# Spreading a short convolution, halving the gates and adding a residual on TensorE in a hybrid decoder step

## The reference, cut to what matters

```
proj = h @ w_in                                  # per token: a conv part (3 x 512) and an RWKV part
y_cv = bg * conv3(cg * hv)                       # short gated convolution, three taps
y_rw = rwkv7(...)                                # a state of 8 heads x 64 x 64, step by step over the tokens
h1   = layer_norm(ALPHA * h + concat(y_cv, y_rw) @ w_o)
# PEER mixer: for each token and each of 8 heads, the best 16 of 16384 experts
hu   = einsum('tkd,td->tk', peer_u[idx], h1)     # 128 gathered rows per token
act  = gelu(hu) * softmax_gate
h2   = layer_norm(ALPHA * h1 + einsum('tk,tkd->td', act, peer_v[idx]))
```

## Time and profile before

| what | value |
|---|---|
| median of 3 runs | 3624.52 us |
| the profiled execution's own time | 3623.29 us |
| its span, first to last instruction | 3621.2 us |
| mean granted TensorE clock | 0.967 of full speed |
| busy PE / DVE / ACT / POOL | 3212.2 / 2425.8 / 808.1 / 2110.1 us |
| HBM read | 1191.03 MB |

### The profile page before, as it was taken

The page is one execution under the profiler, slowest core; times in us unless marked ns, Lnnn a source line. Parts: engine busy times, 40 slices in busy tenths (PEclk is TensorE's granted clock), DMA queues, the critical chain, the costliest instruction groups (busy, mean ns, idle before and its releaser), DMA issues.

```text
span 3621.2 us, 52482 instructions
## 1 busy us (share of the span) xinstructions
PE 3212.2 (89%) x17619; PEld 1702.3 (47%) x17619; DVE 2425.8 (67%) x5758; ACT 808.1 (22%) x1954; POOL 2110.1 (58%) x2172
## 2 busy tenths in 40 slices
PE   4996898599999989998999999999999899989877
PEld 2663565444544454445444544454445444534422
DVE  5463523766776677677767776776677767778795
ACT  2331000122222222222222222222222222222211
POOL 0011800356676666666766666667666676776665
PEclk9997999799999999999999999999999999999999
DMA  4344211789999999999999999999999999999998
GB/s 162 94 128 125 88 38 57 247 301 376 406 409 405 373 407 409 397 373 407 408 407 373 407 409 388 377 407 409 407 373 409 408 406 366 407 408 406 395 379 305
DMA packets 389848, 1218.04 MB, mean 336 GB/s; under 512 B 50194, under 2 KB 97686, under 8 KB 389456
## 3 DMA queue, kind: packets, MB, share of 16 engines
q0 software_dynamic: 302112, 1099.09, 78.2%
q1 hardware_dynamic: 85744, 113.43, 9.1%
q10 hardware_dynamic: 1728, 2.16, 0.2%
HBM read 1191.03 MB, written 31.94 MB: 338 GB/s over the span
## 4 chain that ended last, share of the span: by engine, by line
PE 54%; DMA 16%; DVE 11%; issue 6%; ACT 2%; POOL 2%; DVEq 0%; SPq 0%; POOLq 0%
PE ep_ps L1280 32%; DMA rings<-in_peer_v_dram,idx 10%; PE front_ps L1150 9%; DMA rings<-in_peer_u_dram,idx 6%; PE ep_ps L1328 5%; PE front_ps L1202 3%; PE front_ps L1220 3%; DVE rings L1676 3%; POOL rings L584 2%; ACT L1429 1%; DVE rings L1790 0%; PE front_ps L1211 0%; DVE top_places L1587 0%; DVE top_places L1590 0%; DVE others L1588 0%
## 5 line engine op out<-in xcount | busy, mean ns | idle before, releaser
L1280 PE MATMUL ep_ps<-rings,diag 128*128 128x512 f32 x4096 | 2009.0, 619 | 224.2 <-DMA rings<-in_peer_v_dram,idx 108.9
L584 POOL DMA_INDIRECT rings<-in_peer_u_dram,idx x1024 | 983.1, 960 | 741.3 <-issue 233.7
L1676 DVE CUSTOM_DVE_ANT_0 rings<-rings,x_ps 128x1024 f32<-128x1024 f32 x1024 | 1238.3, 1212 | 96.6 <-DMA rings<-in_peer_u_dram,idx 92.8
L584 POOL DMA_INDIRECT rings<-in_peer_v_dram,idx x1024 | 990.2, 967 | 418.5 <-issue 275.8
L1280 PEld LDWEIGHTS ep_ps<-rings,diag 128*128 128x128 f32 x4096 | 725.4, 193 | 995.7 <-issue 713.1
L1402 ACT ACTIVATE diag<-ident,act_v 128x128 f32<-128x128 f32 x1024 | 348.4, 391 | 190.9 <-PE ep_ps L1280 144.1
L1220 PEld LDWEIGHTS front_ps<-h1T,wq_ring 128*128 128x128 f32 x2304 | 286.3, 196 | 62.9 <-issue 62.9
L1220 PE MATMUL front_ps<-h1T,wq_ring 128*128 128x128 f32 (+1 forms) x2304 | 286.5, 277 | 1.2 <-issue 1.2
L348 PE MATMUL job_ps<-rings,w_ring 128*128 128x352 f32 (+2 forms) x672 | 209.6, 475 | 7.8 <-ACTq L390 3.9
L1328 PE MATMUL ep_ps<-rings 128*128 128x352 f32 x576 | 196.7, 481 | 15.3 <-DVEq L1800 14.0
L1389 ACT ACTIVATE q_T<-front_ps 128x128 f32<-128x128 f32 (+1 forms) x144 | 38.5, 267 | 752.3 <-PE front_ps L1220 752.3
(11 more groups left out here) (349 smaller groups left out, 2880.1 us busy)
## 6 DMA issues: line engine op xcount, KB each, us to landing
wq_ring<-scratch_wq_tiles SPq DMA_DIRECT2D x104, 512.0 KB, 6.8
rings<-in_peer_u_dram,idx POOLq DMA_INDIRECT x1024, 11.3
rings<-in_peer_v_dram,idx POOLq DMA_INDIRECT x1024
ops<-scratch_op_blocks SPq DMA_DIRECT2D x35, 256.0 KB, 9.1
scratch_wq_tiles<-in_w_q_dram SPq DMA_DIRECT2D x16, 512.0 KB, 5.1
w_ring<-in_w_in_dram SPq DMA_DIRECT2D x12, 512.0 KB, 4.0
rings<-in_w_in_dram SPq DMA_DIRECT2D x12, 512.0 KB, 4.2
xrow<-in_x_prompt_dram SPq DMA_DIRECT2D x8, 512.0 KB, 3.7
```

Of the source, the lines that this page charges most:

```text
L584: return pool.indirect_dma_start(out=ring, out_offset=None, in_=table, in_offset=bass.IndirectOffsetOnAxis(ap=index, axis=0))
L1280: mm = pe.matmul(out_ps[:, half, :], diag[:, s % RING, :], v[:, s % RING, half * 512:(half + 1) * 512], start=head == 0 and s == 0, stop=h ...
L1676: dve.tensor_tensor_reduce(u[:, s % RING, :], u[:, s % RING, :], x, 1.0, 0.0, ALU.mult, ALU.add, hu[:, par, s:s + 1]).then_inc(dots, 1)
```

## The change

- The convolution gets its own functions, its weights' ring grows from 5 to 6 tiles, and the 36 units are spread: 5 at the end of `project_phase` (weights loaded there, behind the last projection tiles), 26 in the 87 recurrence slots, 5 in the first 20 slots of `front_to_head_0`. The order of the groups changes so that tiles 9 to 11 are first needed by unit 21.
- GpSimd's sample state is done in slices of 8 rows: 77 steps for 20.
- Gelu and gates are done in two halves of 8 dots. The first half's Gelu is in ScalarE's slot 8, behind the exponential, which moves from slot 4 to slot 7; the first half's gate is in VectorE's slot 10. `diag` for the next turn's slots 0 and 1 is made in slots 14 and 15.
- `res` and its two VectorE passes go. In turn 1 of each block, behind the first sum, TensorE adds ALPHA times the identity times `h`. `finish` copies `out_ps` without an addition. The load of the next `h` also waits for that product.
- The 4 KB per partition of `res` hold the sixth query tile: `NW` = 6.
- The copy of the conv state's last rows moves behind the first heads, and TensorE's gate product no longer waits for it.

```diff
+CONV_EARLY = 5
+CONV_IN_WKV, CONV_IN_NORM = (3 * 29, 26 * KT), (20, (UNITS - CONV_EARLY - 26) * KT)
...
 # project_phase
+            for n in range(N_CONV_W):
+                conv_load(sp, t, d, n)
...
+            for n in range(CONV_EARLY):
+                conv_products(pe, t, n)
...
 # steady_phase
-        NW = 5
+        HALF = TOPK // 2
+        GELU_AT, GATE_AT = HALF, HALF + 2
+        NW = 6
...
+        def front_to_head_0(slot, conv_slot):
+            n = CONV_EARLY + CONV_IN_WKV[0]
             for f in range(NORM, HEAD_SCORED[0]):
                 slot(0, f)
+                conv_slot(n)
+                n += 1
...
 # SyncE
             sp.wait_ge(x_taken, 1)
+            sp.wait_ge(rest_added, 1)
             load_h(1)
...
 # GpSimd
+            def in_parts(out, in0, in1, op):
+                for r in rows(8):
+                    step(pool.tensor_tensor(out[:, r], in0[:, r], in1[:, r], op))
...
 # TensorE, a_turn
                         mm.then_inc(v_used, 1)
+                        if n == 1 and s == 0:
+                            for half in range(2):
+                                mm = pe.matmul(out_ps[:, half, :], alpha_eye[:, :], h[:, half * 512:(half + 1) * 512], start=False, stop=False)
+                            mm.then_inc(rest_added, 1)
...
 # ScalarE, a_turn
+                    i = s + DIAG_LEAD
+                    if i == HALF and sums:
+                        act.wait_ge(act_ready, turn * 2)
+                    if i == TOPK and dots_left:
+                        act.wait_ge(act_ready, turn * 2 + 1)
+                    if i < TOPK and sums or i >= TOPK and dots_left:
+                        diagonal(i)
+                    if s == GELU_AT and dots_left:
+                        gelu(turn, par, 0)
...
-                    if s == 4 and dots_left and not last:
+                    if s == HALF - 1 and dots_left and not last:
                         exp_of(turn + 1, 1 - par)
...
                 if dots_left:
-                    act.wait_ge(dots, (turn + 1) * TOPK)
-                    act.activation(act_v[:, par, :], hu[:, par, :], ACT.Gelu).then_inc(gelu_ready, 1)
+                    gelu(turn, par, 1)
...
 # VectorE
-                    step(dve.tensor_scalar(res[:, :], x, ALPHA, None, ALU.mult))
                     take_rows(new_block)
...
+                    if s == GATE_AT:
+                        gates(turn, par, 0)
...
+                gates(turn, par, 1)
...
-                    dve.tensor_tensor(y[:, :], flat(out_ps[:, :, :]), res[:, :], ALU.add).then_inc(sum_read, 1)
+                    dve.tensor_copy(y[:, :], flat(out_ps[:, :, :])).then_inc(sum_read, 1)
```

More of the change, by code:

```diff
@@ new lines, in conv_copies @@
+def conv_copies(act, t, d, n):
+    unit, old = finished_unit(n), finished_unit(n - 1)
+    if unit is not None and unit % 3 == 0:
+        i = unit // 3
+        if i >= 1:
+            act.wait_ge(t.conv_read, 2 * (i - 1) + 1)
+        act.wait_ge(t.conv_done, unit + 1)
+        act.activation(t.conv.cg, t.out_ps[:, unit % 2, 0:COLS3], ACT.Copy).then_inc(t.cg_ready, 1)
+    if old is not None and old % 3 == 2:
+        i = old // 3
+        c, third = CONV_GROUPS[i]
+        act.wait_ge(t.conv_y_ready, i + 1)
+        act.dma_start(d["y_conv"][:, c, third * COLS3:(third + 1) * COLS3], t.conv.y[:, i % 2, :]).then_inc(t.conv_stored[i % 2], 16)
@@ L484, in _ @@
                     dve.sem_inc(pair_ready, 1)
+            for n in range(CONV_EARLY):
+                conv_vectors(dve, t, n)
 class Stages:
@@ L1119, in a_turn @@
                         gather(pool, u[:, s % RING, :], d["peer_u"][0], index).then_inc(u_landed[s % RING], 16)
+                    if not sums and s == RING:
+                        for stored in t.conv_stored:
+                            pool.wait_ge(stored, 16 * 6)
                     if sums or not own:
@@ L1312, in conv_slot @@
             def conv_slot(n):
[L1314 to L1337, removed]
+                conv_products(pe, t, n)
+            before_norm(chunk_step, conv_slot, front_slot)
+            front_to_head_0(front_slot, conv_slot)
+            front_to_head_1(front_slot)
+            pe.wait_ge(t.conv_chain, CONV_STEPS)
+            pe.wait_ge(t.conv_read, 6 * PAIRS)
+            pe.wait_ge(eye_scaled, 1)
             for c in range(PAIRS):
-                last = pe.transpose(bank[2][0:NS + 2, c * P:(c + 1) * P], t.z_out[:, c, :], t.ident[:, :])
+                last = pe.transpose(out_ps[0:NS + 2, 0, c * P:(c + 1) * P], t.z_out[:, c, :], t.ident[:, :])
             last.then_inc(samp_turned, 1)
-            front_to_head_0(front_slot)
-            front_to_head_1(front_slot)
             over_turns(pe, a_turn, lambda b: None)
@@ L1389, in front_slot, with gelu @@
                     act.activation(q[:, j % 2, 0:rows], bank[2 + j % 2][:, 0:rows], ACT.Copy).then_inc(front_act.at(f"q{j}"), 1)
+            def gelu(turn, par, half):
+                cols = slice(half * HALF, (half + 1) * HALF)
+                act.wait_ge(dots, turn * TOPK + (half + 1) * HALF)
+                act.activation(act_v[:, par, cols], hu[:, par, cols], ACT.Gelu).then_inc(gelu_ready, 1)
             def exp_of(turn, par):
```

326 lines of the change are left out of this document (179 added, 147 removed).

## The result

The changed kernel takes 3535.65 us (median of 4 runs, 3535.28 to 3541.21) against 3625.64 (4 runs): ratio 0.9754, 95% interval 0.9738 to 0.9771. The forecast was 3544.

| stretch | before | after | change | forecast |
|---|---|---|---|---|
| start of the steady phase | 327.58 | 328.24 | +0.7 | +3 |
| recurrence, first product to first norm product | 267.75 | 206.26 | -61.5 | -59.5 |
| from there to the turn of h1 | 30.84 | 45.52 | +14.7 | +14 |
| first gather at | 656.02 | 609.59 | -46.4 | -42.5 |
| first gather to the end of the span | 2965.2 | 2924.4 | -40.8 | -38 |

The account below looks back on a forecast made before the run. Recurrence bound by TensorE's products, norm by VectorE and ScalarE chains, steady blocks by DMA bytes plus losses in TensorE-full turns. Terms: 3623.3 + 3 - 59.5 + 14 - 28 - 10 = 3542.8, beside the median 3544; range 3505 to 3590.

Parts of the forecast that it names:

- (a): End of the projection: five convolution units fill TensorE's idle time there; +3 us, between 0 and +6.
- (b): Recurrence: ten fewer units, no 14 us wait behind GpSimd, +9 given back; -59.5 us, bounds -68 and -38.
- R1: Rival, recurrence: with less cover the VectorE and ScalarE chain shows, some 30 us lost, 3573; chance 0.17.
- (c): Norm: five units in 20 slots, partly hidden in TensorE's idle time; +14 us, bounds 0 and +26.
- (d): Steady turns of seven blocks: turn-end waits go, residual added; -4.06 per block, -28 us, bounds -74 and +14.
- one to one: Steady turns: TensorE time saved counts fully as kernel time, -4.06 us in each of seven blocks.
- (e): Sixth query tile: eight fewer loads of 1.28 us each, in saturated turns; -10 us, or 0 if hidden.
- (f): Items counted at nothing: VectorE's `res` passes, the next load of `h`, the tail's 4.65 us wait, extra instructions.
- R2: Rival, steady turns: turn-end waits are only replaced by others, -28 becomes +14 us, 3586; chance 0.14.
- R3: Rival: no recurrence cover lost (-9), a third of the turns' remaining loss regained (-15), 3520; chance 0.05.
- R4: Rival, slot 10: VectorE waits for ScalarE's Gelu beyond about 20 us, GpSimd's queue stops; 3627 or more; chance 0.05.
- R5: Rival, steady turns: the drain of ScalarE's table switch costs 1 us in 21 turns, 3565; chance 0.03.

## Why the prediction was right, and where its steps were not

The sum came out within 0.3%, and each stretch within 4 us, but several terms were off and made up for each other; that much was luck.

(a) +0.7 for +3: the five units end at 325.26, not after 326.4, and the barrier's tail was 2.98 us.

(b) -61.5 for -59.5, by other terms. Ten units are 80 products at 0.60, -47.7 (twice the 23.83 of the forty early ones), not -53: the 0.66 was a slot's time divided by three, and a slot has a fixed share. TensorE's waits in the stretch fell from 14.03 and 1.31 to 2.14, -13.2. Of the +9 given back only the stall for conv tile 9 is there, 2.14 us and slower products behind it, at 463.0 where the prediction put unit 21. Cover lost: nothing, since no other slot of the recurrence has a wait, so R1 fails. The copy of the conv state's last rows, for which TensorE waited 0.61 us before, is undone in no run by itself. What the prediction missed is that slices and spread don't add: without slices the spread has a wait of 33.5 us, not 14.

(c) +14.7 for +14, where the prediction took the middle between two bounds. Windows from the first norm product to the turn of h1, before and after:

```profile
603.50:634.34 30.84, 19.78 (x49) 8.30 (x47) 16.08 (x20) 3.33 (x5) 0.00 (x0) 0.87 0.45 151
542.47:587.99 45.52, 41.03 (x127) 23.19 (x126) 20.86 (x32) 3.67 (x6) 0.00 (x0) 1.00 0.01 4
```

All 20 slots lie ahead of the turn of h1, and TensorE idled 30.84 - 19.78 = 11.1 us there; the 17.4 of the prediction is the idle time up to the first gather. Of the 11.1, 4.5 are left. So the forty products, about 24 us, hide 6.6 us, and the kernel's own products are some 2.7 us shorter at a granted clock of 1.00 instead of 0.87. From the last mix product to the turn of h1 it is now 587.99 - 576.24 = 11.75 us, with 7.26 us of products in it; the wait before the turn is 4.49 us instead of 7.97.

(d) With five tiles the turns' stretch is 2965.2 - 2935.4 = 29.8 us shorter; forecast 28. The waits changed as said (-2.81, -1.93, and 3.41 to 2.09 for the -1.28). The residual takes 1.88 us for 1.96. Two errors met here. One is a price left out: before, TensorE's products were slower behind each of the three waits of the earlier trace rows, where four records take 3.65, 2.89 and 2.46 us instead of 1.98. Windows behind these waits, in the kernel before:

```profile
1455.50:1460.50 5.00, 5.00 (x22) 2.08 (x23) 1.77 (x5) 0.71 (x3) 1.47 (x2) 0.66 1.03 410
1502.58:1507.50 4.92, 4.92 (x22) 2.41 (x23) 3.51 (x8) 1.12 (x4) 2.82 (x3) 0.65 1.02 408
1546.53:1551.50 4.97, 4.97 (x22) 2.40 (x23) 3.50 (x8) 1.11 (x4) 3.75 (x5) 0.66 1.02 405
```

In each the granted clock was 0.65 to 0.66, so part of the time at the lower level of 1.2 GHz. A third of some 5 us is 1.7 us each, 5.1 per block (an estimate). With it the change frees 6.1 + 5.1 - 1.9 = 9.3 us of TensorE's time in this block; its turns 1 to 3 take 129.4 us for 137.3 before, and 1.3 us saved from the wait for `out_ps` lie ahead of them. The other error, and the step that failed, is "one to one": 29.8/7 = 4.3 us came out, and 3.9 per block in the five middle ones. From there on the DMA sets the pace, as the windows of five blocks show: there less TensorE time gains nothing, and 2 us more of it per block cost nothing. The prediction also put the whole loss of 10.6 us per block down to TensorE; the part in turn 4 isn't, as the rate stayed at 384 there when the wait for h1 went.

(e) 11.0 for 10, as the DMA is the limit there.

(f) The last read of `out_ps` moved from 3598.3 to 3511.0, by 87.3, the span by 87.2: the tail is unchanged.

R2 fails by the vanished `diag` waits. Of R3 no cover was lost, as it said, but no more of the turns' loss came back. R4: from 700 to 3300 us VectorE waits for ScalarE's Gelu at most 3.4 us at a time, far under its 20. R5, timeline of ACT:

```profile
1414.49 1.28 ACT L1518 ACT_TABLE_LOAD   x1
1415.78 0.31 ACT L1518 ACTIVATE head_ex<-head_best,neg_max 128x16 f32<-128x16 f32 x1
...
1416.50 1.28 ACT L1513 ACT_TABLE_LOAD   x1
1417.79 0.21 ACT L1513 ACTIVATE act_v<-hu 128x8 f32<-128x8 f32 x1
```

The pair takes 3.5 us, each function starts 0.01 us behind its load, and no `diag` wait is left between 700 and 3300 us. The drain that the Trainium skill ("ScalarE: Activation LUTs", section "What ACT_TABLE_LOAD costs") adds to a switch is not seen here.

Open: what slows the DMA at full share in turn 4, and the 380 GB/s of turn 1, where GpSimd's gathers wait up to 2.98 us for VectorE's dots and VectorE up to 3.28 us for a TensorE product. Nothing here shows the cause of either.

## What to carry to other kernels

Price an instruction by the difference of two slots, not by one group's time divided by its count, and count the slow records behind a wait with the wait. Judge the limit over a whole block: TensorE had no gap in three turns of eight, and neither more nor less work of its own changed the block. Savings don't add: the halves, the slices, the early units, the norm's units and the sixth tile, each undone alone, cost 47, 33, 18, 16 and 14 us, 127 together, and the change gained 90. After the first saving another engine may be the limit, so say which one it is after each step. Before moving work earlier, look for an arrival that stays at the same time whatever the engine does (here a tile behind another engine's chain on one queue); twelve products moved earlier gained nothing until three loads were moved first.

## What the runs showed of the hardware that was not expected

A VectorE step of 8 columns takes 7 us beside whole GpSimd instructions of 8.8 us, so its length does not matter there; with slices of 1.25 us no TensorE wait was left. In turn 4 the 16 DMA engines show a share of 1.01 at 384 GB/s, against 1.02 at 408 in turn 2: a lower rate is not by itself a sign that they wait. TensorE's clock fell behind waits of 1.93 to 3.41 us, but the length of the wait did not decide it: in the changed kernel, behind a wait of 2.09 us for `out_ps`, four records took 1.99 us at 1394.29, and behind one of 2.08 us they took 3.65 at 2813.06.
